# The next item's first weight piece split ahead of this item's sum, with a fourth split buffer and 8 KB runs for the experts' input weights

## What is computed

```python
h  = x * (1 + scale2) + shift2
x  = LN2(alpha * x + (1 + gate2) * HierMoE(h))      # top-1 of 4 groups, then top-2 of its 8 experts
# for each expert e, over the tokens t routed to it:
a, u = jnp.split(h[t] @ w_e_in[e], 2, axis=-1)      # w_e_in  (32, 1024, 1024)
y    = ((jax.nn.silu(a) * u) @ w_e_out[e]) * gate   # w_e_out (32, 512, 1024)
```

## Time and profile before

| | us |
|---|---|
| median of 3 runs | 1298.1 (1297.53 to 1300.45) |
| the profiled execution | 1297.03 |
| its span | 1295.2 |
| busy: PE / DVE / ACT / POOL | 1104.2 / 894.2 / 634.2 / 267.6 |

### The profile page before, as it was taken

The page is one execution under the profiler, slowest core; times in us unless marked ns, Lnnn a source line. Parts: engine busy times, 40 slices in busy tenths (PEclk is TensorE's granted clock), DMA queues, the critical chain, the costliest instruction groups (busy, mean ns, idle before and its releaser), DMA issues.

```text
span 1295.2 us, 13399 instructions
## 1 busy us (share of the span) xinstructions
PE 1104.2 (85%) x4460; PEld 761.4 (59%) x4460; DVE 894.2 (69%) x974; ACT 634.2 (49%) x639; POOL 267.6 (21%) x227
## 2 busy tenths in 40 slices
PE   5798899888899999999854799999999999999960
PEld 2365568566687666678644556666666666666640
DVE  3868843367464333345596699999999999999957
ACT  3654232222322222332221477777777777777732
POOL 0331940010001000000460741111111111111210
PEclk8798989988999555589785699999999999999985
DMA  9767243153725500024623589999999999999933
GB/s 321 253 238 257 94 152 130 48 169 104 272 73 137 205 0 0 0 98 162 213 68 109 190 336 389 389 393 393 395 395 393 397 391 396 394 390 400 397 110 116
DMA packets 102661, 303.33 MB, mean 234 GB/s; under 512 B 10740, under 2 KB 10788, under 8 KB 102118
## 3 DMA queue, kind: packets, MB, share of 16 engines
q1 hardware_dynamic: 92888, 282.75, 58.6%
q0 software_dynamic: 9744, 20.19, 5.2%
HBM read 299.97 MB, written 14.73 MB: 243 GB/s over the span
## 4 chain that ended last, share of the span: by engine, by line
PE 59%; DVE 18%; DMA 7%; ACT 7%; issue 5%; POOL 4%; SPq 0%; ACTq 0%; POOLq 0%; DVEq 0%
PE banks L1968 9%; PE banks L1976 7%; PE banks L1964 7%; PE banks L1694 6%; PE banks L1700 6%; DVE w_lo L1566 6%; ACT w_hi L973 5%; PE banks L1696 4%; DMA w_raw<-in_w_in 3%; DVE w_lo L1061 3%; PE banks L1727 2%; PE banks L1957 2%; ACT w_hi L816 2%; PE banks L1983 1%; DMA w_raw<-in_w_ada 1%
## 5 line engine op out<-in xcount | busy, mean ns | idle before, releaser
L1566 DVE TENSOR_TENSOR w_lo<-w_raw,w_hi 128x2048 fp32r<-128x2048 f32 x157 | 361.3, 2318 | 36.8 <-ACT w_hi L973 36.8
L973 ACT ACTIVATE w_hi<-w_raw 128x2048 fp32r<-128x2048 f32 x157 | 295.5, 1903 | 0.2 <-issue 0.2
L1061 DVE TENSOR_TENSOR w_lo<-w_raw,w_hi 128x2048 fp32r<-128x2048 f32 x72 | 173.2, 2423 | 137.8 <-ACT w_hi L816 137.7
L816 ACT ACTIVATE w_hi<-w_raw 128x2048 fp32r<-128x2048 f32 x72 | 136.5, 1910 | 210.5 <-PE banks L1700 94.7
L1968 PE MATMUL banks<-w_lo,xT_item 128*128 128x512 f32 x512 | 150.5, 416 | 45.2 <-DVE w_lo L1566 45.2
L1964 PE MATMUL banks<-w_hi,xT_item 128*128 128x512 f32 x512 | 158.9, 433 | 4.2 <-ACT w_hi L973 2.8
L1694 PE MATMUL banks<-w_hi,h_hi 128*128 128x512 f32 x384 | 142.2, 411 | 13.1 <-ACT w_hi L816 12.6
L1968 PEld LDWEIGHTS banks<-w_lo,xT_item 128*128 128x128 f32 x512 | 93.5, 193 | 91.3 <-DVE w_lo L1566 73.1
L1964 PEld LDWEIGHTS banks<-w_hi,xT_item 128*128 128x128 f32 x512 | 96.0, 193 | 39.1 <-issue 14.3
L1976 PE MATMUL banks<-w_raw,hiddenT 128*128 128x512 f32 x248 | 111.4, 592 | 0.0
L1700 PE MATMUL banks<-w_lo,h_hi 128*128 128x512 f32 x384 | 108.2, 404 | 2.4 <-DVE w_lo L1061 2.4
(11 more groups left out here) (438 smaller groups left out, 1579.3 us busy)
## 6 DMA issues: line engine op xcount, KB each, us to landing
w_raw<-in_w_e_in SPq DMA_DIRECT2D x128, 1024.0 KB, 7.3
w_raw<-in_w_e_out SPq DMA_DIRECT2D x64, 1024.0 KB, 6.0
w_raw<-in_w_in SPq DMA_DIRECT2D x32, 1024.0 KB, 9.0
w_raw<-in_w_ada SPq DMA_DIRECT2D x24, 1024.0 KB, 7.2
bias_rows<-in_b_in SPq DMA_DIRECT2D x16, 256.0 KB, 4.8
w_raw<-in_w_ret_proj SPq DMA_DIRECT2D x4, 1024.0 KB, 17.2
w_raw<-in_w_fox_proj SPq DMA_DIRECT2D x4, 1024.0 KB, 18.8
w_raw<-in_w_o SPq DMA_DIRECT2D x4, 1024.0 KB, 5.1
```

Source lines behind the costliest of these rows:

```text
L816: nc.scalar.activation(whi[n % NSPL][:], raw[n % NRAW][:], ACT.Copy).then_inc(hi_done, 1)
L973: nc.scalar.activation(whi[ss][:], raw[j][:], ACT.Copy).then_inc(hi_done, 1)
L1061: V.tensor_tensor(wlo[n % NSPL][:], raw[n % NRAW][:], whi[n % NSPL][:].bitcast(F32), ALU.subtract).then_inc(lo_done, 1)
L1566: V.tensor_tensor(wlo[ss][:], raw[j][:], whi[ss][:].bitcast(F32), ALU.subtract).then_inc(lo_done, 1)
```

## The change

- Two buffers more, `whi_x` and `wlo_x`, for the items alone, in a place that earlier stages used. Piece 3 of an item takes them; pieces 0, 1, 2 keep theirs, piece 4 takes that of piece 1.
- `item_hi(e + 1, 0)` and `item_lo(e + 1, 0)` move: from the start of the next item to ahead of `au_low(e)` and `au_sum(e)` of this one.
- The input weights of the experts go to the partitions in another order: partition p holds the rows 8p to 8p + 7 instead of every 128th row, so that a piece (two rows of 4 KB a partition) is one run of 8 KB in memory. `w_e_out` stays. The features of h2 are permuted to match when DVE writes it (its last add reads with a step of eight elements, from a temporary), and the router's weights are read in the same order.

```diff
+    whi_x = at("w_hi_items", [P, 4, 512], F32R, 57344)
+    wlo_x = at("w_lo_items", [P, 4, 512], F32R, 73728)
+    item_whi, item_wlo = whi + [whi_x], wlo + [wlo_x]
...
-    w_in_e = i["w_e_in"][0].rearrange("e (k p) n -> e p k n", p=P)
+    w_in_e = i["w_e_in"][0].rearrange("e (p k) n -> e p k n", p=P)
...
-    SPLIT_SLOT = (0, 1, 2, 0, 1)
-    SPLIT_BEFORE = (3, 4, 2, 0, 1)
+    SPLIT_SLOT = (0, 1, 2, 3, 1)
     def split_free(e, j):
-        return sub(e if j > 2 else e - 1, SPLIT_BEFORE[j]) + 1
+        return sub(e, 1) + 1 if j == 4 else sub(e - 1, 4 if j == 1 else j) + 1
...
-        pool.dma_start(wr[:, :, 0:NG], i["w_rg"][0].rearrange("(k p) n -> p k n", p=P)).then_inc(wr_in, 16)
+        pool.dma_start(wr[:, :, 0:NG], i["w_rg"][0].rearrange("(p k) n -> p k n", p=P)).then_inc(wr_in, 16)
...
         def item_hi(e, j):
             act.wait_ge(raw_landed[j], 16 * (E0 // NRAW + e))
-            act.wait_ge(used, E0 + j - NSPL + 1 if isinstance(e, int) and e == 1 else split_free(e, j))
-            ss = SPLIT_SLOT[j]
-            nc.scalar.activation(whi[ss][:], raw[j][:], ACT.Copy).then_inc(hi_done, 1)
+            act.wait_ge(used, E0 if isinstance(e, int) and e == 1 and j != 4 else split_free(e, j))
+            nc.scalar.activation(item_whi[SPLIT_SLOT[j]][:], raw[j][:], ACT.Copy).then_inc(hi_done, 1)
...
         def item(e, second):
-            item_hi(e, 0)
             silu(e - 1)
             item_hi(e, 1)
...
             item_hi(e, 3)
             item_hi(e, 4)
+            item_hi(e + 1, 0)
             au_low(sub(e, 3))
             x_high(e + 1)
...
-            st(V.tensor_tensor(ht, xt, m2[0:rows, 1, :], ALU.mult))
-            st.settle()
-            st(V.tensor_tensor(ht, ht, m2[0:rows, 0, :], ALU.add), h2_ready)
+            st(V.tensor_tensor(g1x[0:rows, :], xt, m2[0:rows, 1, :], ALU.mult))
+            st.settle()
+            st(V.tensor_tensor(ht.rearrange("r (k p) -> r k p", k=KD), g1x[0:rows, :].rearrange("r (p k) -> r k p", k=KD),
+                               m2[0:rows, 0, :].rearrange("r (p k) -> r k p", k=KD), ALU.add), h2_ready)
...
         def item_steps(e, second, third):
-            item_lo(e, 0)
             hidden(e - 1)
             item_lo(e, 1)
...
             item_lo(e, 3)
             item_lo(e, 4)
+            item_lo(e + 1, 0)
             au_sum(e)
             x_low(e + 1)
```

More of the change, by code:

```diff
@@ L718, in _ @@
         pool.wait_ge(evacuated, CI["wo0"] + 1)
-        pool.dma_start(wr[:, :, 0:NG], i["w_rg"][0].rearrange("(k p) n -> p k n", p=P)).then_inc(wr_in, 16)
-        pool.dma_start(wr[:, :, NG:], i["w_re"][0].rearrange("(k p) n -> p k n", p=P)).then_inc(wr_in, 16)
+        pool.dma_start(wr[:, :, 0:NG], i["w_rg"][0].rearrange("(p k) n -> p k n", p=P)).then_inc(wr_in, 16)
+        pool.dma_start(wr[:, :, NG:], i["w_re"][0].rearrange("(p k) n -> p k n", p=P)).then_inc(wr_in, 16)
         pool.dma_start(br[:, 0:NG], bcast(i["b_rg"][0], P)).then_inc(wr_in, 16)
@@ L1011, in item @@
             item_hi(e, 4)
+            item_hi(e + 1, 0)
             au_low(sub(e, 3))
             x_high(e + 1)
+        item_hi(1, 0)
         item(1, False)
@@ L1019, in _ @@
             item(e, True)
-        item_hi(n_items, 0)
         silu(n_items - 1)
@@ L1565, in item_lo @@
             dve.wait_ge(hi_done, split_sub(e, j) + 1)
-            V.tensor_tensor(wlo[ss][:], raw[j][:], whi[ss][:].bitcast(F32), ALU.subtract).then_inc(lo_done, 1)
+            V.tensor_tensor(item_wlo[ss][:], raw[j][:], item_whi[ss][:].bitcast(F32), ALU.subtract).then_inc(lo_done, 1)
         def x_low(e):
@@ L1606, in item_steps @@
             item_lo(e, 4)
+            item_lo(e + 1, 0)
             au_sum(e)
             x_low(e + 1)
+        item_lo(1, 0)
         item_steps(1, False, False)
@@ L1614, in _ @@
             item_steps(e, True, True)
-        item_lo(n_items, 0)
         hidden(n_items - 1)
@@ L1963, in product @@
                 for half in range(2):
-                    mm(bank[b0 + half], X[:, k0 + kk, :], whi[ss][:, 2 * kk + half, :], start=(first and kk == 0), stop=False)
+                    mm(bank[b0 + half], X[:, k0 + kk, :], item_whi[ss][:, 2 * kk + half, :], start=(first and kk == 0), stop=False)
             pe.wait_ge(lo_done, n + 1)
@@ L1967, in product @@
                 for half in range(2):
-                    last = mm(bank[b0 + half], X[:, k0 + kk, :], wlo[ss][:, 2 * kk + half, :], start=False, stop=(final and kk == 1))
+                    last = mm(bank[b0 + half], X[:, k0 + kk, :], item_wlo[ss][:, 2 * kk + half, :], start=False, stop=(final and kk == 1))
             last.then_inc(used, 1)
```

## The result

The changed kernel takes 1304.74 us (median of 6 runs, 1302.28 to 1310.81); the kernel before, run beside it, takes 1298.15 us (6 runs). The ratio is 1.0058, 95% interval 1.0032 to 1.0083, so it is slower by 7.5 us (4.2 to 10.8). The profiled execution of after takes 1305.25 us, its span 1303.4, 8.2 us more than the span of before.

What follows compares the result with a forecast made beforehand. The prediction took a 16.38 us chain of waits through the transpose of `hidden` and piece 3 as the bound. Loop and end +10.1 plus h2 +1.4 made +11.5 on 1298.1, so 1309.6 us, range 1299 to 1315.

Steps and rivals of the forecast that it cites:

- What bounds the kernel: Loop over the experts' items: a chain of waits, not busy shares, sets 16.38 us an item; the buffer alone gives nothing.
- The old cycle: PE's transpose of `hidden`, ACT's copy, piece 3's high and low splits, PE's products up to the next transpose: 16.38 us.
- The longer cycle: Three low splits ahead of `au_sum`, then `silu`, piece 1 and the transpose of `hidden`: 16.68 us, +0.30 an item.
- L: The start of DVE's `item_lo(e, 3)`, the low split of piece 3, from which times within an item are counted.
- Over all items: Loop and end: 0.9 at item 1, 29 x 0.30 = 8.7, and 0.5 after the last item, +10.1 us.
- h2: Permuted add of h2 tiles with 32-byte step: 0.7 us each, two of three on the path, +1.4 us (0 to +2.8).
- The sum: Whole kernel: +10.1 for loop and end plus 1.4 for h2 makes +11.5 us, median 1309.6 us.
- the forecast's own range: Whole time 1305 to 1314 us, from the bounds of h2 and 0.1 us an item.
- Cover holds: Rival: PE's own cycle of 16.38 stays and only h2 costs, 1299.5 us; chance 0.14.
- The buffer as the hold: Rival: piece 3's high split begins earlier, DVE's idle 0.56 us an item goes, 17 less, 1282.7 us; faster 0.06.
- Loads late: Rival: piece 0's load lands 0.3 us too late for DVE, 9 us more, 1318.6 us; chance 0.08.
- What I had said the profile would show: Signs: L 16.68 apart, `au_sum` 6.6 after L, waits around piece 1, h2's add 1.9 us, chain naming `silu` and `au_sum`.

Runs made afterwards that it cites:

- piece 3 early: Kernel before plus the two buffers, 8 KB runs and permuted h2, with piece 3's splits issued ahead of `hidden_high` and `hidden_low`; ratio 0.9951.
- the two parts measured apart: Against the kernel before: order and buffers alone, ratio 1.0061 (+7.9 us); 8 KB runs and permuted h2 alone, ratio 1.0025 (+3.3 us).
- the two later sums: `au_sum` at L + 6.61 in the changed kernel (1304.74 us) and L + 7.75 with 1024 more elements subtracted ahead of it (1343.72 us).
- half a split ahead: Changed kernel with only half of the next piece 0's low split ahead of `au_sum`, the rest behind `x_low`; one run, 1300.32 us.
- the fourth pair alone: Kernel before with only the two extra buffers added, order and rows of `w_e_in` as before; ratio 0.9998.
- piece 1 ahead of `silu`: Changed kernel with piece 1's high split issued ahead of `silu` on ACT and its low split ahead of `hidden` on DVE; ratio 1.0029 to before.
- the sum ahead: Changed kernel with DVE's low split of the next piece 0 moved behind `au_sum` and `x_low`; ratio 1.0008 to the kernel before.
- the last kernel: As piece 3 early, with the gather of item 3's tokens moved ahead of POOL's last two operations on x; ratio 0.9934.

## Why the prediction was right

**What bounds the kernel.** Right. The old cycle holds the loop at 16.38: cut by itself it gives 15.38 (piece 3 early), while the buffer gives nothing and the 8 KB runs give nothing at the old step.

**The longer cycle.** Right in mechanism and in size, point by point:

| | predicted | measured in after |
|---|---|---|
| `au_sum` starts | L + 6.64 | L + 6.61 |
| ACT's high split of piece 1 done | L + 10.32 | L + 10.29 |
| low part of piece 1 done | L + 12.63 | L + 12.61 |
| PE begins that product | L + 12.68 | L + 12.67 |
| step | 16.68 | 16.67 |
| point from which it decides, in `au_sum` | 0.30 earlier | 0.30 earlier by a line, between 0 and 1.07 by the rows |

**Over all items.** From item 2's L to item 31's I had 29 x 0.30 = 8.7; it is 8.4 (759.23 to 1242.62 is 483.39, against 475.00 in the earlier trace rows). From item 1's `au_sum` to item 2's L I had 10.04; it is 759.23 - 749.17 = 10.06. Ahead of that sum the forecast was off: I charged one more low split at its usual 2.20 us there, but from item 1's `hidden_low` to its `au_sum` after takes 13.06 us and before 9.83 (738.57 to 748.40), 3.23 more, since the splits go on beside POOL's work, where two of them take 8.85. So item 1 costs 1.94 us and not 0.9. At the end `hidden_low` starts 0.44 later after L than in the earlier trace rows (13.66 against 13.22); I had 0.5.

```profile
736.11 0.42 DVE L1585 TENSOR_TENSOR hiddenT<-banks,hiddenT 128x256 fp32r<-128x256 f32 x1
...
740.39 8.85 DVE L1568 TENSOR_TENSOR w_lo<-w_raw,w_hi 128x2048 fp32r<-128x2048 f32 x2
749.17 1.21 DVE L1577 TENSOR_TENSOR au_sum<-banks,au_low 64x1024 f32<-64x1024 f32 x1
...
759.23 2.29 DVE L1568 TENSOR_TENSOR w_lo_items<-w_raw,w_hi_items 128x2048 fp32r<-128x2048 f32 x1 [0.39 <-ACT w_hi_items L974]
...
1242.62 2.29 DVE L1568 TENSOR_TENSOR w_lo_items<-w_raw,w_hi_items 128x2048 fp32r<-128x2048 f32 x1 [0.39 <-ACT w_hi_items L974]
...
1256.28 0.41 DVE L1585 TENSOR_TENSOR hiddenT<-banks,hiddenT 128x256 fp32r<-128x256 f32 x1
```

**h2.** One add of the first tile and the add to the logits behind PE, first of before, then of after:

```profile
673.96 1.22 DVE L1421 TENSOR_TENSOR h<-h,mod_prompt 128x1024 f32<-128x1024 f32 x1
...
690.20 0.23 DVE L1437 TENSOR_TENSOR logits<-banks,b_router 128x72 f32<-128x72 f32 x1 [3.59 <-PE banks L1914]
```

```profile
671.96 1.99 DVE L1422 TENSOR_TENSOR h<-affine_tmp,mod_prompt 128x1024 f32<-128x1024 f32 x1
...
689.74 0.23 DVE L1439 TENSOR_TENSOR logits<-banks,b_router 128x72 f32<-128x72 f32 x1 [2.74 <-PE banks L1916]
```

The add takes 0.77 us more (I took 0.7). The first add starts 2.00 us earlier in this execution, the logits only 0.46 earlier: 1.54 us on the path, and I had 1.4. That is no accident of one execution: from this add to the logits it is 16.24 or 16.25 us in the four profiles with the old h2, and 17.78 to 17.82 in the ten with the permuted one. The Trainium skill, "SBUF — State Buffer", section "Door 1: The DMA port swizzle (why [64,N] ≈ [32,N])", by which both inputs pay, would have made 2.8 of my price for one. The trace doesn't bear out a doubled price: 0.77 us is what the add as a whole pays, and how it divides between the inputs wasn't measured.

**The sum.** Here the prediction was 4 us high, 11.5 against 7.5 (4.2 to 10.8). In the two profiled executions the stretches that the change touches cost 12.2 us, near the forecast, and what I hadn't written down is that the others need not stay the same. From span to span the 8.2 us are:

| stretch | us |
|---|---|
| up to h2 | -2.0 |
| h2 to the logits | +1.54 |
| logits to the first `hidden_low` | -2.0 |
| first to second `hidden_low` | +1.94 |
| the next 29 steps | +8.56 |
| last step and what is behind | +0.16 |

The second -2.0 can be read in part. Products that PE made at a granted clock of 0.50 in before (716.30 to 718.20 and 735.10 to 737.20) had 0.91 and 1.00 in after. Two rows of before, and the same two products of after, which are 0.70 and 0.88 us shorter:

```profile
716.32 1.91 PE L1964 MATMUL banks<-w_hi,xT_item 128*128 128x512 f32 x4
...
735.10 2.08 PE L1968 MATMUL banks<-w_lo,xT_item 128*128 128x512 f32 x4 [1.20 <-DVE w_lo L1566]
```

```profile
715.87 1.21 PE L1966 MATMUL banks<-w_hi,xT_item 128*128 128x512 f32 x4
...
733.90 1.20 PE L1970 MATMUL banks<-w_lo,xT_item 128*128 128x512 f32 x4 [1.20 <-DVE w_lo L1568]
```

Such stretches differ from execution to execution: the h2 add starts anywhere from 669.6 to 675.4 us in the fourteen profiles of this study, and the first `hidden_low` from 734.4 to 743.6. A sum built on one execution carries that. Whether the medians of the timed runs differ by the same 4 us isn't shown; the two parts measured apart made 11.2. So the size of the loop's loss was understood, but that the total lies in the stated range owes something to luck: the forecast's own range missed it by 0.3 us, and the wider one took it in only because it reached down to a rival.

**Rivals.** Cover holds: refuted by the step of 16.67 and the wait for piece 1. It was near: 0.30 us by the line through the two later sums, and at most 1.07, since with half a split ahead the step is 16.37. The buffer as the hold: refuted by the fourth pair alone. Loads late: refuted for the changed kernel, where they land in 6.6 us (median; 7.3 before) and no high split waits for one.

**What I had said the profile would show.** Steps, `au_sum`, DVE's 1.12 us of waiting, ACT's 2.62, PE's weights waiting for piece 1 and h2's add all came. The chain of waits was said to name `silu` and `au_sum`; it doesn't.

## What to carry to other kernels

When work moves ahead of a result that others wait for, follow what is queued behind that result on each engine until the loop closes, and compare that cycle with the one that holds now: here the sum could be put off by some 1.66 us (from L + 4.65 to 6.31) for nothing, the change put it off by 1.96, and the 0.30 beyond was paid in every item. A buffer or longer runs pay only where the wait that they remove is the last one; the 8 KB runs gave 0.23 us an item once the loads were the bound, and nothing before. And a stall removed from the order of a hand-written queue goes to the next operation behind the same slow one, unless the slow one itself moves.

## What the runs showed of the hardware

**The clock falls for a moment in the loop.** In the profiles of all five changed kernels with a step of 16.37 single items take 1.55 us more, in one step of 17.92 or two of 17.46 and 16.84. In the kernel with piece 1 ahead of `silu`, PE:

```profile
832.38 1.20 PE L1970 MATMUL banks<-w_lo_items,xT_item 128*128 128x512 f32 x4 [1.14 <-DVE w_lo_items L1568]
...
834.31 1.97 PE L1966 MATMUL banks<-w_hi,hiddenT 128*128 128x512 f32 x4
836.08 1.91 PE L1970 MATMUL banks<-w_lo,hiddenT 128*128 128x512 f32 x4
...
852.23 1.19 PE L1966 MATMUL banks<-w_hi,hiddenT 128*128 128x512 f32 x4
```

1.97 and 1.91 us against 1.19 and 1.10 an item later are the two levels, 1.2 and 2.4 GHz: the granted clock is 0.53 from 836 to 838 us and 1.00 from 850 to 854. Ahead of the fall PE had stood 1.14 us for piece 3, in one stretch. It happened three times in that profile, twice in that of half a split ahead, and never in the profiles with a step of 16.67 or 17.81. The profile of before has nearly the same waiting (1.05 us) and no such item, so the waiting alone doesn't decide it. What does stays open. Three of them are 4.7 us, so they may be a part of the ratios 1.0025 and 1.0029, which came out high. Against that, the kernel with the fourth pair alone has two or three of them in its profile and measured 0.9998, and the one with the sum ahead has three and measured 1.0008. That wasn't tested. Nor do the records show whether other executions of before have such items; if they do, the change, whose step of 16.67 shows none, is spared them, and its loss is smaller than its steps alone would say.

**POOL beside DVE.** The issue of the gather, first in before, then in after:

```profile
912.39 0.94 POOL L741 DMA_INDIRECT x_item<-scratch_h,slot_token  x1 [5.32 <-PE banks L1957]
```

```profile
914.53 2.27 POOL L743 DMA_INDIRECT x_item<-scratch_h,slot_token  x1 [5.17 <-PE banks L1959]
```

In after it begins beside DVE's low splits, and ends 0.90 us behind the start of `au_sum` at 915.90, as if it had begun only with it. In before it runs beside `au_sum`, which reads a bank of PSUM. POOL's 12.25 and 12.96 us above seem to be the same for whole operations, beside DVE's splits, which take their usual 2.27 us there. It goes the other way too: the split that starts at 742.12 in the last kernel, just behind the start of a POOL operation of 2.37 us (741.86), takes 4.26 us instead of 2.29. The Trainium skill, "SBUF — State Buffer", section "Who interferes with whom", says that a DVE instruction with two inputs in SBUF contends with a GpSimd one that reads SBUF, by an exclusive lock. The trace agrees: 12.25 us against 4.42 for the same operation in before, where DVE's splits were stretched too.
